# FFN loop: five mixed pairs of eight with a mixed one last, down columns copied out by ScalarE and added by GpSimd's transfers

## The chip, the cores and the metric

The kernel runs on one core of one Trainium2 chip. The metric is the device time of one execution in microseconds; several executions are timed and their median is given. A profile of one execution comes with it.

## What is computed

One block of a hybrid encoder on 256 tokens with 2048 channels: a mixer sub-layer (retention heads and a diagonal state-space group), then a dense SwiGLU feed-forward (FFN), all in float32:

```python
SEQ, D_MODEL, D_FF = 256, 2048, 5632
    x = x + mix @ w_out[l]
    h = rmsnorm(x, norm_ffn_g[l])
    x = x + (jax.nn.silu(h @ w_gate[l]) * (h @ w_up[l])) @ w_down[l]
    return rmsnorm(x, norm_final_g)
```

The change touches the last product line, the FFN.

## The kernel before

**High and low parts.** Every float32 product is made of three matmuls on rounded parts: high times high, high times low, low times high. A weight chunk (128 x 1024, 512 KB) is loaded by SyncE's queue into one of six slots (`raw`, `raw_more`), ScalarE (ACT) copies it rounded into `w_hi` (L550), VectorE (DVE) writes the rest, `raw - w_hi`, into `w_lo` (L947), and TensorE (PE) multiplies. `w_hi` and `w_lo` have four slots, so ACT may write chunk c when PE has finished chunk c-4. The semaphores `high_done`, `low_done` and `pe_done` count these steps; `ready(n)` on PE waits for `low_done` ahead of every chunk.

**The loop.** `D_FF` is cut into 11 blocks of 512. A turn (`turn(j)`, written for each engine; 10 turns) has 24 chunks. Chunks 0 to 15 are the **gate phase**: eight pairs of a gate chunk and an up chunk of the next block. Chunks 16 to 23 are the **down phase**: four columns of 512 outputs, two chunks each, of the block whose activations (`ffT`) the turn before prepared. Twelve matmuls of 512 columns per down chunk.

**Plain and mixed pairs.** The string `UNITS` says for each of the pairs 0 to 7 whether it is plain (C) or mixed (S). A plain pair takes eight block products, 24 matmuls (`plain_unit`). A mixed pair takes seven, 21 matmuls (`mixed_unit`), by sums of blocks in the way of Strassen and Winograd: first nine matmuls on three blocks of `w_hi`/`w_lo` (banks P1, P2, P3), then twelve on sums of weight blocks in `mix_hi`/`mix_lo` (banks P4 to P7). For a mixed pair DVE makes the sums (`mix_sums`, three operations, L1312 to L1317), then w_lo of one and a half chunks, then `mix_lo` (L1323, 128 x 2048); ACT makes `w_hi` of one and a half chunks and `mix_hi` (two of L559). The tile `mix` has one buffer, `mix_hi` and `mix_lo` have two. Sums of the activations (`sA`, `sB`, `sC`) are made once, ahead of the loop, by `combos`, `combo_high`, `combo_low`.

**From products to activations.** After the last mixed pair ACT copies bank P1 into `mix` (`first_product`), DVE adds P6 and P7 (`first_sums`, L1328 and L1330), and after the whole gate phase `last_sums` adds P5 and then P2 to P4 (L1336, L1339). ACT takes the silu, DVE multiplies (`ff`), turns 32 x 32 blocks (`turn_blocks`), and 16 small transfers of GpSimd's queue move them (`move`, L424); they come back as `ffT_hi` (ACT) and `ffT_lo` (DVE, L1371) in the gate phase of the next turn.

**Down columns.** The columns of the down phase use two pairs of PSUM banks in turn. When a column's two chunks are done, DVE adds both banks to the residual `x2` in SBUF (`down_add`, L1381, counted by `cols_added`), and PE may use the banks again. Each engine's queue is in program order; the order is written out by hand in `turn(j)`.

In the texts below D is the moment at which PE starts chunk 16, the first of a down phase, and T the moment at which it starts chunk 0.

Of the kernel before, what the change touches and what calls it, by code (L numbers as in the profile page):

```python
# [40 lines left out]
NCOL = 512  # L41
# [7 lines left out]
SPL = 4  # L49
# [16 lines left out]
UNITS = "CSCSSCSC"  # L66
# [3 lines left out]
B_P2, B_P3, B_P4, B_P5, B_P1, B_P6, B_P7 = range(7)  # L70
# [80 lines left out]
def build(nc, A, out):  # L151
# [20 lines left out]
    with ctx:  # L172
# [80 lines left out]
        for part, x in enumerate((m["sB_hi"], m["sB_lo"])):  # L253
            s_mixed[part] += [x[:, i] for i in range(2)]
        wbT, dec, sT = (m[k] for k in ("wbT", "dec", "sT"))
# [55 lines left out]
        d_cols_pool = [sem(f"d_cols_pool{i}") for i in range(COLS_MOVED)]  # L311
        d_last, d_last_pool = sem("d_last"), sem("d_last_pool")
# [221 lines left out]
        def _(act):  # L534
# [17 lines left out]
            def mix_high(c, turn=None):  # L552

                q = mixed_at(c)
                for half_, step in ((slice(0, 2), 1), (slice(2, 4), 3)):
                    act.wait_ge(S["mix_step"], count(turn, 3 * NM, 3 * q + step))
                    if turn is not None and step == 1:
                        act.wait_ge(S["mix_free"], count(turn, NM, q))
                    nc.scalar.activation(mix_hi[:, q % 2, half_], mix[:, half_], ACT.Copy).then_inc(S["mix_high"], 1)  # L559
# [1702 lines left out]
```

## Time and profile before

| | |
|---|---|
| median of 3 runs | 1094.39 us (1093.68 to 1094.54) |
| the profiled execution, its own time | 1094.19 us |
| its span, first to last instruction | 1092.1 us |
| busy: PE, DVE, ACT, GpSimd | 1080.7, 936.1, 601.1, 189.9 us |
| granted clock of TensorE, mean | 0.998 of full speed |

Busy time is the time in which an engine has an instruction at work; PE's matmuls overlap (a new one starts some 0.227 us after the one before, and each row lasts 0.39 us). A row of the timeline with "x2" merges two instructions. In square brackets stand the idle time ahead of an instruction and what ended it. Times count from the start of the span.

### The profile page before, as it was taken

How to read it: one execution, taken by the hardware profiler on the slowest of the kernel's cores; microseconds unless marked ns; L12 is line 12 of the kernel's file. 1: busy time of each engine (PE TensorE's matmuls, PEld its weight loads, DVE VectorE, ACT ScalarE, POOL GpSimd, SP SyncE). 2: the span in 40 equal slices, each digit the busy share in tenths (PEclk: the TensorE clock that was granted, in tenths of full speed). 3: DMA queues.
4: the chain of work that ended last, by engine and by line, in shares of the span. 5: the costliest groups of instructions: out<-in, count | busy, mean ns of one | idle time of the engine just before them, and what ended most of it. 6: DMA issues, size and time to landing. Idle time of an engine off the chain costs nothing.

```text
span 1092.1 us, 15574 instructions
## 1 busy us (share of the span) xinstructions
PE 1080.7 (99%) x5386; PEld 892.1 (82%) x5386; DVE 936.1 (86%) x1043; ACT 601.1 (55%) x738; POOL 189.9 (17%) x322
## 2 busy tenths in 40 slices
PE   9999999999999999999999999999999999999997
PEld 7878778888988888888888888888888888888886
DVE  7999998754875788989898998989899898989987
ACT  7569544445753565545555464655546465555544
POOL 7130143320100320311030302003030300303011
PEclk9999999999999999999999999999999999999999
DMA  9884588864665677666576666658566665757662
GB/s 360 286 232 147 179 235 242 268 191 150 212 218 187 205 221 229 214 206 212 197 230 220 185 228 204 201 191 241 200 210 214 207 206 182 229 192 231 214 213 113
DMA packets 123802, 232.18 MB, mean 213 GB/s; under 512 B 12016, under 2 KB 19568, under 8 KB 123120
## 3 DMA queue, kind: packets, MB, share of 16 engines
q1 hardware_dynamic: 113392, 215.10, 61.1%
q0 software_dynamic: 9952, 15.62, 5.4%
q10 hardware_dynamic: 416, 0.92, 0.2%
q8 instruction: 25, 0.41, 0.2%
q14 instruction: 17, 0.14, 0.0%
HBM read 218.09 MB, written 5.11 MB: 204 GB/s over the span
## 4 chain that ended last, share of the span: by engine, by line
PE 80%; DVE 13%; DMA 3%; issue 2%; ACT 1%; DVEq 0%; POOL 0%; SPq 0%; POOLq 0%; ACTq 0%
PE ps L1787 36%; PE ps L1751 31%; DVE w_lo L941 4%; PE ps L1778 3%; PE ps L1771 3%; PE ps L1775 3%; DMA raw<-in_w_in 2%; DVE w_lo L947 1%; DVE wb L1074 1%; DVE wb L1072 1%; ACT w_hi L544 1%; DVE wb_t L1073 1%; PE ps L2095 1%; PE ps L2096 1%; PE ps L2097 1%
## 5 line engine op out<-in xcount | busy, mean ns | idle before, releaser
L550 ACT ACTIVATE w_hi<-raw 128x1024 fp32r<-128x1024 f32 (+1 forms) x166 | 156.7, 955 | 191.2 <-PE ps L1787 117.7
L544 ACT ACTIVATE w_hi<-raw 128x1024 fp32r<-128x1024 f32 x135 | 142.7, 1060 | 154.0 <-DMA raw<-in_w_in 53.2
L941 DVE TENSOR_TENSOR w_lo<-raw,w_hi 128x1024 fp32r<-128x1024 f32 x136 | 163.8, 1220 | 63.7 <-ACT w_hi L544 63.1
L424 POOL DMA_DIRECT2D ff_moved<-ff_turned x184 | 97.0, 536 | 601.7 <-DVE ff_turned L1365 543.3
L947 DVE TENSOR_TENSOR w_lo<-raw,w_hi 128x1024 fp32r<-128x1024 f32 (+1 forms) x166 | 176.3, 1088 | 23.7 <-ACT w_hi L550 22.9
L550 ACT ACTIVATE w_hi<-raw_more 128x1024 fp32r<-128x1024 f32 x82 | 84.5, 1054 | 54.9 <-PE ps L1751 36.5
L947 DVE TENSOR_TENSOR w_lo<-raw_more,w_hi 128x1024 fp32r<-128x1024 f32 x82 | 97.4, 1218 | 8.4 <-ACT w_hi L550 8.4
L559 ACT ACTIVATE mix_hi<-mix 128x1024 fp32r<-128x1024 f32 x80 | 83.5, 1056 | 21.9 <-DVE mix L1312 15.2
L1323 DVE TENSOR_TENSOR mix_lo<-mix,mix_hi 128x2048 fp32r<-128x2048 f32 x40 | 91.4, 2285 | 0.0
L1751 PE MATMUL ps<-w_hi,ffT_hi 128*128 128x512 f32 x320 | 85.6, 389 | 0.0
L1751 PE MATMUL ps<-w_lo,ffT_hi 128*128 128x512 f32 x320 | 85.6, 389 | 0.0
L1751 PE MATMUL ps<-w_hi,ffT_lo 128*128 128x512 f32 x320 | 85.5, 389 | 0.0
L1751 PEld LDWEIGHTS ps<-w_hi,ffT_hi 128*128 128x128 f32 x320 | 60.1, 188 | 12.5
L1751 PEld LDWEIGHTS ps<-w_lo,ffT_hi 128*128 128x128 f32 x320 | 60.1, 188 | 12.5
L1751 PEld LDWEIGHTS ps<-w_hi,ffT_lo 128*128 128x128 f32 x320 | 60.1, 188 | 12.5
L1787 PE MATMUL ps<-w_hi,h2B_hi 128*128 128x512 f32 x160 | 52.8, 391 | 0.1
L1787 PE MATMUL ps<-w_lo,h2B_hi 128*128 128x512 f32 x160 | 52.9, 392 | 0.0
L1787 PE MATMUL ps<-w_hi,h2B_lo 128*128 128x512 f32 x160 | 52.9, 391 | 0.0
L1787 PE MATMUL ps<-w_lo,actA_hi 128*128 128x512 f32 x160 | 52.5, 389 | 0.0
L1787 PE MATMUL ps<-w_hi,actA_hi 128*128 128x512 f32 x160 | 52.5, 389 | 0.0
L1787 PE MATMUL ps<-w_hi,actA_lo 128*128 128x512 f32 x160 | 52.5, 389 | 0.0
L1312 DVE TENSOR_TENSOR mix<-raw 128x1024 f32<-128x1024 f32 x40 | 48.8, 1220 | 1.4 <-DMA raw<-in_w_up 0.9
(362 smaller groups left out, 2238.4 us busy)
## 6 DMA issues: line engine op xcount, KB each, us to landing
raw<-in_w_in SPq DMA_DIRECT2D x79, 512.0 KB, 5.4
raw<-in_w_gate SPq DMA_DIRECT2D x68, 512.0 KB, 3.9
raw<-in_w_up SPq DMA_DIRECT2D x68, 512.0 KB, 4.6
raw<-in_w_down SPq DMA_DIRECT2D x46, 512.0 KB, 4.1
raw_more<-in_w_down SPq DMA_DIRECT2D x42, 512.0 KB, 4.5
raw<-in_w_out SPq DMA_DIRECT2D x32, 512.0 KB, 4.1
raw_more<-in_w_gate SPq DMA_DIRECT2D x20, 512.0 KB, 4.5
raw_more<-in_w_up SPq DMA_DIRECT2D x20, 512.0 KB, 5.5
```

The lines of the kernel that those rows point to most:

```text
L424: eng.dma_start(moved[32 * b:32 * b + 32, :, a].rearrange("p t k j -> p t (k j)"), turned[32 * a:32 * a + 32, b].rearrange("p t k j -> p t ...
L544: nc.scalar.activation(w_hi[:, n % SPL], raw[:, n % RAW], ACT.Copy).then_inc(S["high_done"], 1)
L550: nc.scalar.activation(w_hi[:, c % SPL, at], raw_of(c)[:, at], ACT.Copy).then_inc(S["high_done"], 1)
L559: nc.scalar.activation(mix_hi[:, q % 2, half_], mix[:, half_], ACT.Copy).then_inc(S["mix_high"], 1)
L941: tt(w_lo[:, n % SPL], raw[:, n % RAW], w_hi[:, n % SPL].bitcast(F32), ALU.subtract).then_inc(S["low_done"], 1)
L947: tt(w_lo[:, c % SPL, at], raw_of(c)[:, at], w_hi[:, c % SPL, at].bitcast(F32), ALU.subtract).then_inc(S["low_done"], 1)
L1312: tt(mix[:, 0:2], b12.unsqueeze(1).to_broadcast([P, 2, NCOL]), blocks[:, 0::3], ALU.subtract).then_inc(S["mix_step"], 1)
L1323: tt(mix_lo[:, q % 2], mix[:], mix_hi[:, q % 2].bitcast(F32), ALU.subtract).then_inc(S["mix_low"], 1)
L1751: ins = mm(ps[:, banks + t], blocks[k][kind == 1][:, tok], w[:, s, at], start=first and kind == 0 and k == 0, stop=last and kind == 2 and ...
L1771: mm(ps[:, banks + t], blocks[k][0][:, tok], w_hi[:, s, at], start=first and k == 0, stop=False)
L1775: mm(ps[:, banks + t], blocks[k][1][:, tok], w_hi[:, s, at], start=False, stop=False)
L1787: ends[bank] = mm(ps[:, bank], x[kind == 1], w[b], start=kind == 0 and bank in fresh, stop=kind == 2 and bank in done)
```

## The change

`UNITS` becomes CSCSSCSS: pair 7 is mixed now as well, so five of eight are. Its sums of activations get tiles of their own (`sD`), and since NM is odd now, the buffers of `mix_hi`/`mix_lo` are chosen by `q % NM % 2`. The banks are dealt out anew: P1 and bank 7 are one pair of down columns, P6 and P7 the other (`COL_BANKS`). DVE no longer adds down columns; ACT copies each into `col_a` or `col_b` (`column_out`), and GpSimd's queue issues a transfer that adds it to `x2` in SBUF. The semaphore `cols_added` is called `col_done` and counts the copies, and `d_added` counts the landings of the adding transfers. `first_sums` waits for the whole gate phase (`mix_free`), and PE waits for `p1_ready` ahead of chunk 16 and for `sum_step` ahead of chunk 18 only. ACT's turn 0 is written out ahead of the loop.

```diff
-UNITS = "CSCSSCSC"
+UNITS = "CSCSSCSS"
-B_P2, B_P3, B_P4, B_P5, B_P1, B_P6, B_P7 = range(7)
+B_P2, B_P3, B_P4, B_P5, B_P6, B_P7, B_P1 = range(7)
+COL_BANKS = ((B_P1, 7), (B_P6, B_P7))
...
             def first_product(j):
 
-                act.wait_ge(S["mix_free"], j * NM + (NM + 1))
+                act.wait_ge(S["pe_done"], j * TURN + (LOOP0 + 2 * MIXED[-1] + 1))
...
+            def column_out(j, col, first=False):
+
+                act.wait_ge(S["pe_done"], j * TURN + (LOOP0 + 2 * GRP + 2 * col + 2))
+                if not (first and col < 2):
+                    act.wait_ge(d_added[col % 2], j * 32 + 16 * (col // 2))
+                nc.scalar.activation(col_out[col % 2][:], column_psum(col), ACT.Copy).then_inc(S["col_done"], 1)
...
+                    if c in (2 * GRP + 5, 2 * GRP + 7, TURN + 1):
+                        column_out(j, (c - 2 * GRP - 5) // 2, first)
+                    if c == TURN + 3:
+                        column_out(j, 3, first)
...
             def first_sums(j):
 
                 dve.wait_ge(S["p1_ready"], j + 1)
+                dve.wait_ge(S["mix_free"], j * NM + (NM + 1))
...
-            def down_col(chunks, before, c):
-
-
-                dve.wait_ge(S["pe_done"], chunks)
-                dve.wait_ge(S["cols_added"], before)
-                b0 = 6 - 2 * (c % 2)
-                cols = x2[:, :, NCOL * c:NCOL * (c + 1)]
-                tt(cols, ps[:, b0:b0 + 2], cols, ALU.add).then_inc(S["cols_added"], 1)
...
             for j in range(FG - 1):
                 pool.wait_ge(S["turned"], j + (COLS_MOVED + 1))
                 move(pool, PAIRS, ff_turned, ff_moved, d_moved)
-            pool.wait_ge(S["turned"], COLS_MOVED + FG)
-            pool.wait_ge(S["ffT_lo_ready"], FG - 1)
-            move(pool, PAIRS[8:], ff_turned, ff_moved, d_last_pool)
+                for col in range(4):
+                    pool.wait_ge(S["col_done"], 4 * j + 9 + col)
+                    pool.dma_start(x2[:, :, NCOL * col:NCOL * (col + 1)], col_out[col % 2][:], accum_op=ALU.add
+                                   ).then_inc(d_added[col % 2], 16)
...
                 for c in range(2 * GRP, TURN):
                     col, k = divmod(c - 2 * GRP, 2)
                     if c == 2 * GRP:
                         pe.wait_ge(S["ffT_lo_ready"], j + 1)
+                        pe.wait_ge(S["p1_ready"], j + 1)
+                    if c == 2 * GRP + 2:
                         pe.wait_ge(S["sum_step"], j * 4 + 2)
```

Two places in the order of the instructions matter below. The first is DVE's queue at the hand-over from the gate phase to the down phase, in the loop's body. The first row is the w_lo of chunk 17, and the two rows behind the sums are those of chunks 18 and 19. Before:

```order
L947 TENSOR_TENSOR w_lo<-raw_more,w_hi 128x1024 [waits high_done]
L1328 TENSOR_TENSOR mix<-ps,mix 128x512 [waits p1_ready]
L1330 TENSOR_TENSOR mix<-ps,mix 128x512 [waits sum_step]
L1336 TENSOR_TENSOR mix<-mix,ps 128x2x512 [waits sum_step,pe_done]
L1339 TENSOR_TENSOR mix<-ps,mix 128x1536 [waits sum_step]
L946 REGISTER_ALU
L947 TENSOR_TENSOR w_lo<-raw,w_hi 128x1024 [waits high_done]
L946 REGISTER_ALU
L947 TENSOR_TENSOR w_lo<-raw,w_hi 128x1024 [waits high_done]
```

The changed kernel has the same instructions there, under other line numbers:

```order
L977 TENSOR_TENSOR w_lo<-raw_more,w_hi 128x1024 [waits high_done]
L1364 REGISTER_ALU [waits p1_ready]
L1365 TENSOR_TENSOR mix<-ps,mix 128x512 [waits mix_free]
L1366 ISA
L1367 TENSOR_TENSOR mix<-ps,mix 128x512 [waits sum_step]
L1372 REGISTER_ALU [waits pe_done]
L1373 TENSOR_TENSOR mix<-mix,ps 128x2x512 [waits sum_step]
L1375 REGISTER_ALU
L1376 TENSOR_TENSOR mix<-ps,mix 128x1536 [waits sum_step]
L976 REGISTER_ALU
L977 TENSOR_TENSOR w_lo<-raw,w_hi 128x1024 [waits high_done]
```

The order has not moved, but the first of the four sums waits for `mix_free` now, which the last matmul of pair 7 gives; before, the first wait of the four for the end of pair 7 was that of the third (`pe_done`, L1336).

The second place is ACT's queue in the down phase, between the silu and the next turn. The rows of `w_hi` are chunks 20 to 23 and then 0 and 1 of the next turn. The changed kernel, in the turn that is written out:

```order
L885 ACTIVATE ff_act<-mix,rstd 128x512
L569 ACTIVATE w_hi<-raw 128x1024 [waits pe_done,d_raw2]
L569 ACTIVATE w_hi<-raw 128x1024 [waits pe_done,d_raw3]
L893 ACTIVATE col_a<-ps 128x1024 [waits pe_done]
L569 ACTIVATE w_hi<-raw_more 128x1024 [waits pe_done,d_raw4]
L569 ACTIVATE w_hi<-raw_more 128x1024 [waits pe_done,d_raw5]
L893 ACTIVATE col_b<-ps 128x1024 [waits pe_done]
L569 ACTIVATE w_hi<-raw 128x1024 [waits pe_done,d_raw0]
L569 ACTIVATE w_hi<-raw 128x1024 [waits pe_done,d_raw1]
L893 ACTIVATE col_a<-ps 128x1024 [waits d_added0,pe_done]
```

The rows of L893 are new, each behind the `w_hi` of two chunks; the third waits for the landing of the first column's adding transfer as well. The fourth stands behind the two `mix_hi` of the next turn's pair 1.

## Rows read from the trace of the kernel before

**Rows 1.** The page, part 1: busy us of each engine (share) xinstructions.

```profile
PE 1080.7 (99%) x5386; PEld 892.1 (82%) x5386; DVE 936.1 (86%) x1043; ACT 601.1 (55%) x738; POOL 189.9 (17%) x322
```

**Rows 2.** The chain that ended last: start us, us, what, one turn.

```profile
560.24 41.08 PE ps L1787 x180
601.32 21.76 PE ps L1751 x96
```

**Rows 3.** Windows, one turn: us, busy (x) of five engines, PEclk, DMA share, GB/s.

```profile
560.24:623.08 62.84, 62.84 (x277) 51.84 (x277) 56.90 (x54) 34.02 (x36) 8.41 (x16) 1.00 0.65 208
```

**Rows 4.** Timeline of PE, one turn: start us, us, what.

```profile
590.82 0.62 PE L1787 MATMUL ps<-w_hi,h2B_hi 128*128 128x512 f32 x2
...
595.69 0.62 PE L1787 MATMUL ps<-w_hi,h2B_hi 128*128 128x512 f32 x2
...
601.16 1.07 PE L1751 MATMUL ps<-w_hi,ffT_hi 128*128 128x512 f32 x4
...
606.60 1.07 PE L1751 MATMUL ps<-w_hi,ffT_hi 128*128 128x512 f32 x4
```

**Rows 5.** Groups of DVE in the same turn, shapes apart.

```profile
L1381 DVE TENSOR_TENSOR x<-ps,x 128x1024 f32<-128x1024 f32 x4 | 4.9, 1216 | 0.0
```

**Rows 6.** Timeline of DVE at the same hand-over, from 597 us.

```profile
597.42 0.68 DVE L1328 TENSOR_TENSOR mix<-ps,mix 128x512 f32<-128x512 f32 x1
598.14 0.69 DVE L1330 TENSOR_TENSOR mix<-ps,mix 128x512 f32<-128x512 f32 x1
601.36 1.22 DVE L1336 TENSOR_TENSOR mix<-mix,ps 128x1024 f32<-128x1024 f32 x1 [2.53 <-PE ps L1787]
602.61 1.76 DVE L1339 TENSOR_TENSOR mix<-ps,mix 128x1536 f32<-128x1536 f32 x1
604.29 2.35 DVE L947 TENSOR_TENSOR w_lo<-raw,w_hi 128x1024 fp32r<-128x1024 f32 x2
```

**Rows 7.** Timeline of DVE in turn 0, at pair 4.

```profile
452.68 1.82 DVE L947 TENSOR_TENSOR w_lo<-raw,w_hi 128x1024 fp32r<-128x1024 f32 x2
```

**Rows 8.** Timeline of PE at the same place.

```profile
454.04 0.39 PE L1787 MATMUL ps<-mix_lo,actA_hi 128*128 128x512 f32 x1
...
455.13 0.39 PE L1787 MATMUL ps<-w_hi,sB_hi 128*128 128x512 f32 x1
```

**Rows 9.** Timeline of DVE, pair 6 of a later turn.

```profile
646.42 1.22 DVE L1312 TENSOR_TENSOR mix<-raw 128x1024 f32<-128x1024 f32 x1
...
649.01 1.82 DVE L947 TENSOR_TENSOR w_lo<-raw,w_hi 128x1024 fp32r<-128x1024 f32 x2
650.75 2.29 DVE L1323 TENSOR_TENSOR mix_lo<-mix,mix_hi 128x2048 fp32r<-128x2048 f32 x1
652.95 1.22 DVE L947 TENSOR_TENSOR w_lo<-raw,w_hi 128x1024 fp32r<-128x1024 f32 x1
```

**Rows 10.** Timeline of ACT, around the start and end of a gate phase.

```profile
623.65 1.99 ACT L559 ACTIVATE mix_hi<-mix 128x1024 fp32r<-128x1024 f32 x2
625.84 1.07 ACT L550 ACTIVATE w_hi<-raw_more 128x1024 fp32r<-128x1024 f32 x1 [0.19 <-PE ps L1787]
...
653.86 1.06 ACT L550 ACTIVATE w_hi<-raw 128x1024 fp32r<-128x1024 f32 x1 [1.66 <-PE ps L1787]
```

**Rows 11.** Timeline of DVE ahead of turn 0.

```profile
423.45 0.28 DVE L1286 TENSOR_TENSOR s_sum<-h_sum 128x128 f32<-128x128 f32 x1
...
424.71 1.22 DVE L941 TENSOR_TENSOR w_lo<-raw,w_hi 128x1024 fp32r<-128x1024 f32 x1
...
428.50 0.42 DVE L1299 TENSOR_TENSOR sC_lo<-s_sum,sC_hi 128x256 fp32r<-128x256 f32 x1
...
432.12 1.23 DVE L1312 TENSOR_TENSOR mix<-raw 128x1024 f32<-128x1024 f32 x1 [0.94 <-DMA raw<-in_w_up]
```

**Rows 12.** DMA issues of the execution: KB each, median us to landing.

```profile
u_scratch<-uT POOLq DMA_DIRECT2D x2, 512.0 KB, 5.1
...
x<-in_x_tok SPq DMA_DIRECT2D x1, 2048.0 KB, 9.0
```

More of the change, by code:

```diff
@@ L254, in build @@
             s_mixed[part] += [x[:, i] for i in range(2)]
+        for part in range(2):
+            s_mixed[part].append(s_last[part][:])
         wbT, dec, sT = (m[k] for k in ("wbT", "dec", "sT"))
@@ L363, in mixed_pair, with combo_parts @@
             return c % TURN < 2 * GRP and c % TURN // 2 in MIXED
-        def column_combos(c):
-            one = 2 * c if 2 * c in MIXED else 2 * c + 1
-            return MIXED.index(one), PLAIN.index(4 * c + 1 - one), one - 2 * c
+        def combo_parts(c):
+            first, parts = 0, []
+            for u in (2 * c, 2 * c + 1):
+                width = 4 if u in MIXED else 2
+                to = [s_mixed[part][MIXED.index(u)] if u in MIXED else s_plain[part][PLAIN.index(u)] for part in range(2)]
+                parts.append((s_sum[:, first:first + width], to))
+                first += width
+            return parts
         def act_block(kb, part):
@@ L557, in mix_high @@
                     if turn is not None and step == 1:
[L558 to L559 removed]
+                        act.wait_ge(S["mix_free"], count(turn, NM, q + (NM % 2 and q == NM)))
+                    nc.scalar.activation(mix_hi[:, q % NM % 2, half_], mix[:, half_], ACT.Copy).then_inc(S["mix_high"], 1)
             def pair_high(c, turn=None):
@@ L883, in _, with turn @@
                 pair_high(c)
-            def turn(j, last=False):
+            def turn(j, first=False, last=False):
                 for c in range(SPL, TURN + SPL):
@@ L902, in turn @@
                                              ).then_inc(S["ffT_hi_ready"], 1)
-            with act.Fori(0, FG - 2) as j:
+            turn(0, first=True)
+            with act.Fori(1, FG - 2) as j:
                 turn(j)
@@ L1277, in combos @@
             def combos(c):
-                _, _, one = column_combos(c)
                 pair = h_sum[:].rearrange("p (u k) (t s) -> p u k t s", u=2, t=TOK)
-                (a11, a21), (a12, a22) = ([pair[:, one, k, t] for t in range(TOK)] for k in range(2))
-                plain = pair[:, 1 - one]
-                dve.wait_ge(S["h_summed"], 3 * c + 1)
+                done = sum(1 + 2 * (u in MIXED) for u in range(2 * c)) - c
+                dve.wait_ge(S["h_summed"], done + 1)
                 if c:
@@ new lines, in combos @@
+                for i, (sums, _) in enumerate(combo_parts(c)):
+                    if 2 * c + i in MIXED:
+                        a11, a21, a12, a22 = (pair[:, i, k, t] for k in range(2) for t in range(TOK))
+                        tt(sums[:, 0], a21, a22, ALU.add).then_inc(S["h_summed"], 1)
+                        tt(sums[:, 2], a21, a11, ALU.subtract)
+                        mixed.append((sums, a11, a12))
+                    else:
+                        last = tt(sums, pair[:, i, :, 0], pair[:, i, :, 1], ALU.subtract)
@@ L1294, in combo_low @@
+                for i, (sums, a11, _) in enumerate(mixed):
+                    dve.wait_ge(S["h_summed"], done + 2 + i)
+                    tt(sums[:, 1], sums[:, 0], a11, ALU.subtract).then_inc(S["h_summed"], 1)
+                for i, (sums, _, a12) in enumerate(mixed):
+                    dve.wait_ge(S["h_summed"], done + 2 + len(mixed) + i)
+                    last = tt(sums[:, 3], a12, sums[:, 1], ALU.subtract)
+                last.then_inc(S["s_summed"], 1)
             def combo_low(c):
-                i, k, _ = column_combos(c)
```

95 lines of the change are left out of this document (47 added, 48 removed).

## The prediction

> **What bounds the kernel now.** I read the page first: PE is busy 99% of the span, DVE 86%, ACT 55% [rows 1]. So a stretch of PE's work saved is worth its full length only as long as DVE, the next engine, keeps its deadlines. The chain of work that ended last says the same for the loop: one turn after another is two pieces, both PE, 41.08 us of gate phase and 21.76 us of down phase, with nothing between [rows 2]. The windows of that turn put 56.90 us of DVE's work and 34.02 us of ACT's into 62.84 us, and the sixteen DMA engines are busy 0.65 of it, 41 us [rows 3]. PE does not wait in these turns; DVE is ahead of it by a margin that differs from place to place. The question is therefore which margin the change uses up, and I walk through one turn for that.
>
> **What is removed: three matmuls a turn.** Pair 7 goes from 24 matmuls to 21. Pair 6 is a mixed pair on the same activations (h2B) and lasts from 590.82 to 595.69, 4.87 us; pair 7, plain, lasts to 601.16, 5.47 us [rows 4]. That is 0.60 us. At the usual step of a matmul (5.44 us for the 24 of the first down column, 601.16 to 606.60 [rows 4], 0.227 each) it would be 0.68. I take 0.64 a turn, 6.4 us in ten turns, with 6.0 and 6.8 as ends.
>
> **DVE's work.** It loses four down adds of 1.22 us, 4.9 us a turn [rows 5]. It gains the mixed pair's work. For pair 6 that is 2.59 us of sums (646.42 to 649.01), 1.74 us of w_lo and 2.20 us of `mix_lo` (starts at 649.01, 650.75, 652.95) [rows 9], 6.53 us, where a plain pair needs two w_lo of 1.2 us [rows 9]. Net +4.1 -4.9: DVE's sum hardly moves and PE's turn gets 0.6 shorter. By sums alone the change would pay in full.
>
> **The hand-over to the down phase.** This is where it does not. Today `first_sums` runs at 597.42 and 598.14, while PE is in pair 7; DVE then idles 2.53 us until pair 7's end lets `last_sums` start at 601.36, 0.20 us after PE's chunk 16 starts (D = 601.16) [rows 4, 6]. The two last sums take until 604.29, then come the w_lo of chunks 18 and 19, the first done at about 605.51. PE wants chunk 18 at 606.60: a margin of 1.1 us.
> With pair 7 mixed, P6 and P7 end with pair 7's last matmul, so the first of the four sums cannot start before D + 0.20. The chain behind it is serial and each step is in the rows: 0.72 (597.42 to 598.14), 0.72 again for the second (the same operation, followed by one that waits for it), 2.93 for the two last sums (601.36 to 604.29), 1.22 for w_lo 18: D + 0.20 + 0.72 + 0.72 + 2.93 + 1.22 = D + 5.79. PE wants it at D + 5.44. The work that hid the first two sums was pair 7; now nothing does.
> What such a lateness costs is seen once in the trace, in turn 0 at pair 4: w_lo was complete at 452.68 + 1.82 = 454.50 [rows 7]. PE's last matmul before it started at 454.04, so the next chunk was due at 454.27 and its third matmul at 454.72; it started at 455.13 [rows 8]. Late by 0.23, lost 0.41: the loss is the lateness plus 0.18. Here: 0.35 + 0.18 = **0.53 us a turn**, 5.3 us in ten turns. I take 0.45 to 0.65 as its ends, for a step may differ by a few hundredths. PE cannot make up for it later, since everything behind is its own work.
> Other deadlines there hold. `p1_ready`: P1 ends after nine of pair 7's 21 matmuls, so ACT's copy of one bank can start 2.7 us (twelve matmuls) ahead of D. Chunk 19 is due at D + 8.7, its w_lo is ready at D + 6.9. The columns of P6 and P7 are free at about D + 1.7, before chunk 18.
>
> **Pair 7 as a mixed pair.** DVE is free at 652.95, after pair 6's `mix_lo` [rows 9]. Sums to 655.5, w_lo to 657.3, `mix_lo` to 659.5. PE starts pair 7 at 595.69 + 62.84 = 658.53 and its second half nine matmuls later, about 660.6. Margins 1.2 and 1.1 us: tight, but no wait. ACT does not spoil it: its `w_hi` 15 starts at 653.86 by PE's release [rows 10], now half as long, and the two `mix_hi` end a microsecond behind the sums, before DVE needs them. Then w_lo 16, `ffT_lo` and w_lo 17 take DVE to about 662.9, PE's new D being 663.4: in time.
>
> **ACT's copies.** Four a turn; the 128 x 1024 copy is 1.06 us where the source is SBUF [rows 10], and I take the same from PSUM. With `mix_hi` (two, 2.0 us) less half a `w_hi` ACT gains some 6 us on 34 in 62: its sum is no bound. Three copies stand where it waited for PE anyway. The fourth stands behind the `mix_hi` of pair 1, which end at 625.64; the `w_hi` of chunk 4 started at 625.84 [rows 10] and now starts at 626.7. The w_lo of chunk 5 comes when PE releases its slot, as before, and so costs nothing. PE needs the fourth column's banks only in pair 1's second half, at T + 7.5; the copy is over at T + 3.8.
>
> **The adding transfers.** Nothing in the trace adds while it moves, so I bound it. Below: a plain transfer of the same 512 KB from GpSimd's queue lands in 5.1 us; above: one of four times the bytes in 9.0 us [rows 12]. An adding transfer reads source and target and writes, so I take 7 us, between the two. The first deadline is the third column's copy, which waits for the first column's landing. Column 0 is complete at D + 5.4, and ACT, after silu and two `w_hi`, has copied it by D + 9; ACT wants to copy column 2 at about D + 18, after PE's chunk 21 and its own `w_hi`. So 9 us, and 1.5 more in which ACT would be idle: hidden. The fourth waits for the second with 12 us. In GpSimd's queue the 16 moves of the next block now stand behind the fourth add, some 13 us later than today; they end by about T + 15, and `ffT_hi` reads them at T + 32: hidden.
> The Trainium skill, "DMA: Bandwidth & Descriptors", section "Issuing engines are not separate DMA queues", says that transfers of all queues interleave on the same 16 engines, so the adds compete with the weights. By the fit in its section on the SWDGE path (2.0 us plus bytes over 436 GB/s) half a megabyte would be an estimate of 3.2 us, and 4.4 with the target's read; no run here shows an adding transfer yet. By it the rival of slow adds would be out; by the rows above it is open.
>
> **Ahead of turn 0.** The last group of sums has two mixed pairs: eight small operations where five take 1.26 us, and a w_lo of 512 columns where 256 take 0.33 (428.50 to the next operation), so DVE gets about 0.7 us later there. It waits only 0.94 us for a transfer, and that is released by the w_lo just before, so it shifts too [rows 11]. In turn 0 PE does wait for DVE at pair 4 [rows 8], so this comes through, and at pair 7 DVE has less reserve than later (a mixed pair costs it 6.5 us, PE 4.9), worth 0.2 to 1. I take +1.1 for both, ends 0.4 and 1.8.
>
> **The sum.** Against the profiled execution's own 1094.19 us: -6.4 (matmuls) +5.3 (wait at chunk 18) +1.1 (turn 0) = 1094.2. That execution stands 0.2 below the median of the runs, so I say 1094.3: no change. The ends of the terms give -6.8 + 4.5 + 0.4 = -1.9 and -6.0 + 6.5 + 1.8 = +2.3, so 1092.3 to 1096.6 for this case, practically all within 0.2% (2.2 us), which is also about what a measurement of this kernel can tell from no change. The tail after the last turn is the same work, and its waits for the landings have over 8 us.
>
> **The rivals.**
> - *The wait does not come* (the sums are quicker out of PSUM, or PE's deadline is later than I read it). For it: 0.35 us of lateness is small against a turn. Against it: every step is a row of this kernel, and 0.4 us in a chain of 5.8 would have to vanish. Time: 1094.2 - 5.3 = 1088.9.
> - *The margins at the mixed pairs go too.* Pair 7's 1.1 us, and those of pair 4, which follows pair 3 the same way. If weights land a microsecond or two later under the adds, the sums of pair 1 start later and DVE, which runs without a pause from there to pair 6, hands it on. Price: 0.4 us a turn, 4 us: 1098.
> - *Slow adds, the case on the slower side.* One mechanism: ACT, in order, waits for the first column's landing before its third copy, and all `w_hi` behind it wait. It decides from about 10.5 us from copy to landing, or from (62.2 - 41)/4 = 5.3 us of all sixteen DMA engines for each add. At 12.5 us of landing it costs 2 us a turn, 20 us: 1114.
> - That the adds take work from DVE but DVE's sum is no bound is not a rival but part of the forecast: taking them away shortens nothing by itself.
>
> **How the numbers follow.** Forecast 0.46, no wait 0.19, margins gone 0.17, slow adds 0.14; 0.04 for something between (half the wait) that ends faster. Range 1088.5 to 1100: it takes in the first three and leaves out the slow adds and a little more. Faster: 0.19 + 0.04 + 0.01 of the forecast's low end = 0.24. Slower: 0.17 + 0.14, less 0.01 that stays within = 0.30. Within 0.2%: 0.46.
>
> **What would show it.** In the changed kernel's trace PE should idle, ten times, about 0.5 us at the third down chunk behind DVE's w_lo, and four sums should stand in one row right behind the first down matmul. Gate phases should be 40.4 to 40.5 us long, the down phases 22.3. The adds should land in 5 to 9 us and no ACT row should name them as releaser. I am wrong if the down phase is 21.8 us still, if a wait for `mix_lo` or w_lo stands at pair 4 or 7 of every turn, or if ACT waits for the adds.

## The result: 0.4% slower, the loop as forecast and the tail not

| | before | after |
|---|---|---|
| median of 6 runs each | 1094.38 us (1093.68 to 1094.81) | 1099.25 us (1098.30 to 1100.84) |
| ratio, with 95% interval | | 1.0041 (1.0030 to 1.0051) |
| profiled execution: its own time, span | 1094.19, 1092.1 us | 1099.47, 1097.5 us |

The kernel is 4.9 us slower. The time lies inside the range on record, but the forecast case, no change, did not come, and the kernel is on the side that had 0.30. In the changed kernel the names of the lines are: L1774 down matmuls (L1751 before), L1810 mixed gate matmuls (L1787), L977 `w_lo` (L947), L1365 to L1376 the four sums, L893 `column_out`, L1730 the adding transfer.

Busy time of the changed kernel, the page's part 1, answers to [rows 1]:

```profile
PE 1079.6 (98%) x5356; PEld 887.2 (81%) x5356; DVE 935.9 (85%) x1046; ACT 647.8 (59%) x798; POOL 240.7 (22%) x362
```

Thirty matmuls are gone, three in each of ten turns, and DVE's sum has not moved. One turn in the chain that ended last (start us, us, what), beside [rows 2]:

```profile
560.29 40.41 PE ps L1810 x177
...
600.73 0.70 DVE mix L1365
...
602.18 1.23 DVE mix L1373
...
605.11 1.22 DVE w_lo L977
...
606.38 16.61 PE ps L1774 x72
```

What the reader is to see: the gate phase shrank from 41.08 to 40.41 us, and what was one unbroken piece of 21.76 us of PE is now interrupted after two chunks. The chain leaves PE at 600.7, goes through DVE's sums and the w_lo of chunk 18, and returns to PE at 606.38. PE's timeline there, beside [rows 4], says the same from PE's side:

```profile
600.53 1.07 PE L1774 MATMUL ps<-w_hi,ffT_hi 128*128 128x512 f32 x4
...
606.38 1.20 PE L1774 MATMUL ps<-w_hi,ffT_hi 128*128 128x512 f32 x4 [0.25 <-DVE w_lo L977]
```

Chunk 18 starts at D + 5.85 (606.38 - 600.53) where 5.44 was due. That is 0.41 us late, and the first four matmuls behind it take 0.13 longer than the row of chunk 16 (1.20 against 1.07). The idle time in the brackets (0.25) is smaller than the loss, for the matmul before still counts as busy in a part of the wait. From 600.70, the end of the gate phase in the chain, to the next gate phase at 623.00 it is 22.29 us, 0.53 more than 21.76.

The same turn in the windows (us, busy of five engines, PEclk, DMA share, GB/s), beside [rows 3]:

```profile
497.60:560.29 62.69, 62.44 (x274) 51.21 (x274) 56.87 (x54) 38.68 (x42) 13.37 (x20) 1.00 0.81 242
```

ACT has 4.7 us more, GpSimd 5.0, and the sixteen DMA engines went from 0.65 to 0.81 of the turn. PE waits for none of these.

To place the 4.9 us I cut both spans at the same four points: the start of the loop (433.87 and 432.96 us), the start of turn 1 (497.24 and 497.43), the moment at which the tail's first chunk was due (1062.80 and 1061.99), and the end. All are starts of matmuls in PE's timeline, which stand 0.16 us ahead of the chain's marks (601.16 there is 601.32 in the chain of [rows 2]).

| us | before | after | difference |
|---|---|---|---|
| up to the loop | 433.87 | 432.96 | -0.9 |
| turn 0 | 63.37 | 64.47 | +1.1 |
| nine more turns | 565.56 | 564.56 | -1.0 |
| the tail | 29.3 | 35.5 | +6.2 |
| span | 1092.1 | 1097.5 | +5.4 |

These are single executions, and the first two rows vary between executions: in the profiles of e1, e4 and e8 (below), whose kernels are the changed one up to the tail, the loop starts at 433.95, 433.56 and 432.98 us and turn 0 lasts 64.87, 64.37 and 65.60. The nine turns do not vary so (564.53 us in e1), and 6.2 us are well beyond this scatter. So turns and tail have to be told apart: the turns did what was forecast, and the loss lies in the last 36 us. In the tail block 10 of the FFN is finished: eight more chunks of down weights against `ffE_hi`/`ffE_lo`, and the final norm, for which 1 MB `g_final` is loaded. PE's timeline of the changed kernel there:

```profile
1063.52 1.17 PE L1774 MATMUL ps<-w_hi,ffE_hi 128*128 128x512 f32 x4 [1.37 <-issue]
...
1077.39 0.50 PE L1763 MATMUL ps<-w_hi,ffE_hi 128*128 128x512 f32 x1 [2.71 <-DVE x L1555]
```

Two waits. The first chunk starts 1.5 us after it was due (1061.99), the fifth 2.9 us after (1074.52). What DVE and ACT waited for ahead of them, from their timelines:

```profile
1061.10 1.06 ACT L930 ACTIVATE ffE_hi<-ff_moved 128x1024 fp32r<-128x1024 f32 x1 [2.32 <-DMA ff_moved<-ff_turned]
...
1077.15 1.06 ACT L569 ACTIVATE w_hi<-raw 128x1024 fp32r<-128x1024 f32 x1 [6.57 <-DMA raw<-in_w_down]
```

```profile
1073.77 2.36 DVE L977 TENSOR_TENSOR w_lo<-raw_more,w_hi 128x1024 fp32r<-128x1024 f32 x2 [7.40 <-DMA g_final<-in_g_final]
```

Everything late there is a landing: the moved blocks, `g_final`, the weights of the last chunks. The DMA issues of the last turn and the tail (KB each, median us to landing), before and then after:

```profile
raw_more<-in_w_down SPq DMA_DIRECT2D x2, 512.0 KB, 6.2
g_final<-in_g_final SPq DMA_DIRECT2D x1, 1024.0 KB, 8.6
...
ff_moved<-ff_turned SPq DMA_DIRECT2D x8, 32.0 KB, 2.3
```

```profile
x<-col_a POOLq DMA_DIRECT2D x2, 512.0 KB, 9.2
raw_more<-in_w_down SPq DMA_DIRECT2D x2, 512.0 KB, 8.6
g_final<-in_g_final SPq DMA_DIRECT2D x1, 1024.0 KB, 13.4
ff_moved<-ff_turned SPq DMA_DIRECT2D x8, 32.0 KB, 4.2
```

The windows of the same stretch, again before and then after:

```profile
1046.00:1062.80 16.80, 16.80 (x76) 13.89 (x75) 15.15 (x16) 7.95 (x8) 4.22 (x8) 1.00 0.77 240
1062.80:1078.00 15.20, 15.20 (x69) 12.59 (x68) 12.50 (x14) 7.75 (x12) 0.00 (x0) 1.00 0.29 117
```

```profile
1046.00:1063.50 17.50, 16.15 (x72) 13.01 (x71) 11.43 (x13) 10.56 (x11) 8.00 (x11) 1.00 0.90 214
1063.50:1078.40 14.90, 12.17 (x52) 9.79 (x53) 6.87 (x7) 5.16 (x5) 1.19 (x1) 1.00 0.94 278
```

From 1046 to 1078 the DMA engines had 17.3 us of work (0.77 x 16.80 + 0.29 x 15.20) and have 29.8 (0.90 x 17.50 + 0.94 x 14.90) in 32.4 us. They are nearly full. The page's part 3 (queue: packets, MB, share of 16 engines) gives the price of one adding transfer; first the lines of before, then of after:

```profile
q1 hardware_dynamic: 113392, 215.10, 61.1%
q0 software_dynamic: 9952, 15.62, 5.4%
```

```profile
q1 hardware_dynamic: 113392, 215.10, 59.5%
q0 software_dynamic: 20832, 36.59, 15.8%
```

0.158 x 1097.5 less 0.054 x 1092.1 is 114 us for 40 transfers, 2.9 us of all sixteen engines for each. That is the upper end: q1's time fell by 14 us for the same bytes, so both queues together grew by 100 us, 2.5 for each. Four of them are 10 to 11.4 us, most of the 12.5 that this stretch has more.

A third piece is PE's own. Two windows of the changed kernel, the stretch without a matmul and the one behind it:

```profile
1074.68:1077.39 2.71, 0.00 (x0) 0.00 (x1) 2.68 (x5) 0.24 (x1) 0.00 (x0) 1.00 0.74 260
1077.39:1082.50 5.11, 5.11 (x15) 4.06 (x16) 5.11 (x6) 4.61 (x10) 0.00 (x0) 0.67 0.01 3
```

After 2.71 us in which PE stood, the granted clock of the next 5.1 us is 0.67: part of the stretch ran at the lower of TensorE's two levels, 1.2 instead of 2.4 GHz. Eight matmuls between 1078.58 and 1081.99 follow each other at 0.43 us instead of 0.23, 1.6 us lost. Late start 1.5, late fifth chunk 2.9 and the clock 1.6 make 6.0 of the tail's 6.2 us. The clock's part is not the same in every execution, as e2 and e3 show below.

### The profile page after: what moved, and what is told of

Read it like the earlier page. It is cut to its first block, busy times and chain, and to the rows that moved or that the text cites. A ratio compares the mean times of both kernels' runs of the same rounds, so it can differ in the third digit from the quotient of the medians.

```text
span 1097.5 us, 15723 instructions
## 1 busy us (share of the span) xinstructions
PE 1079.6 (98%) x5356; PEld 887.2 (81%) x5356; DVE 935.9 (85%) x1046; ACT 647.8 (59%) x798; POOL 240.7 (22%) x362
## 3 DMA queue, kind: packets, MB, share of 16 engines
q1 hardware_dynamic: 113392, 215.10, 59.5%
q0 software_dynamic: 20832, 36.59, 15.8%
HBM read 218.09 MB, written 5.11 MB: 203 GB/s over the span
## 4 chain that ended last, share of the span: by engine, by line
PE 75%; DVE 15%; issue 4%; DMA 4%; ACT 1%; SPq 0%; DVEq 0%; POOL 0%; POOLq 0%; ACTq 0%
PE ps L1810 33%; PE ps L1774 27%; PE ps L1801 3%; PE ps L1794 3%; PE ps L1798 3%; DVE w_lo L971 3%; DVE w_lo L977 2%; DMA raw<-in_w_in 2%; DMA g_final<-in_g_final 1%; DVE mix L1373 1%; DVE mix_lo L1359 1%; DVE mix L1367 1%; DVE mix L1365 1%; PE ps L2120 1%; PE ps L2121 1%
## 5 line engine op out<-in xcount | busy, mean ns | idle before, releaser
L569 ACT ACTIVATE w_hi<-raw 128x1024 fp32r<-128x1024 f32 (+1 forms) x166 | 150.0, 927 | 141.3 <-PE ps L1810 84.2
L977 DVE TENSOR_TENSOR w_lo<-raw,w_hi 128x1024 fp32r<-128x1024 f32 (+1 forms) x166 | 171.0, 1056 | 30.7 <-ACT w_hi L569 30.1
L1359 DVE TENSOR_TENSOR mix_lo<-mix,mix_hi 128x2048 fp32r<-128x2048 f32 x50 | 114.3, 2285 | 10.8 <-ACT mix_hi L578 10.8
L443 POOL DMA_DIRECT2D ff_moved<-ff_turned x184 | 102.5, 865 | 78.3 <-DVE ff_turned L1402 77.9
L578 ACT ACTIVATE mix_hi<-mix 128x1024 fp32r<-128x1024 f32 x100 | 103.6, 1054 | 22.4 <-DVE mix L1348 13.4
L1730 POOL DMA_DIRECT2D x<-col_a x20 | 24.4, 1222 | 398.5 <-ACT col_a L893 393.3
L977 DVE TENSOR_TENSOR w_lo<-raw_more,w_hi 128x1024 fp32r<-128x1024 f32 x82 | 98.2, 1217 | 12.3 <-DMA g_final<-in_g_final 7.4
L1774 PE MATMUL ps<-w_hi,ffT_hi 128*128 128x512 f32 x320 | 86.8, 393 | 2.9 <-DVE w_lo L977 2.9
L1774 PE MATMUL ps<-w_hi,ffT_lo 128*128 128x512 f32 x320 | 85.6, 390 | 0.0
L1774 PE MATMUL ps<-w_lo,ffT_hi 128*128 128x512 f32 x320 | 85.6, 389 | 0.0
L1774 PEld LDWEIGHTS ps<-w_hi,ffT_hi 128*128 128x128 f32 x320 | 59.3, 188 | 18.9 <-DVE w_lo L977 6.2
L1774 PEld LDWEIGHTS ps<-w_hi,ffT_lo 128*128 128x128 f32 x320 | 60.1, 188 | 12.6
L1774 PEld LDWEIGHTS ps<-w_lo,ffT_hi 128*128 128x128 f32 x320 | 60.1, 188 | 12.5
L1348 DVE TENSOR_TENSOR mix<-raw 128x1024 f32<-128x1024 f32 x50 | 61.0, 1221 | 1.7 <-DMA raw<-in_w_up 0.8
L1810 PE MATMUL ps<-w_hi,actA_hi 128*128 128x512 f32 x160 | 52.7, 390 | 0.1
L1810 PE MATMUL ps<-w_lo,actA_hi 128*128 128x512 f32 x160 | 52.5, 389 | 0.0
L1810 PE MATMUL ps<-w_hi,actA_lo 128*128 128x512 f32 x160 | 52.5, 389 | 0.0
L1794 PE MATMUL ps<-w_hi,actA_hi 128*128 128x512 f32 x160 | 44.6, 401 | 0.1
L1794 PE MATMUL ps<-w_hi,actB_hi 128*128 128x512 f32 x160 | 44.3, 399 | 0.0
```

The lines of the kernel that those rows point to most:

```text
L443: eng.dma_start(moved[32 * b:32 * b + 32, :, a].rearrange("p t k j -> p t (k j)"), turned[32 * a:32 * a + 32, b].rearrange("p t k j -> p t ...
L569: nc.scalar.activation(w_hi[:, c % SPL, at], raw_of(c)[:, at], ACT.Copy).then_inc(S["high_done"], 1)
L578: nc.scalar.activation(mix_hi[:, q % NM % 2, half_], mix[:, half_], ACT.Copy).then_inc(S["mix_high"], 1)
L977: tt(w_lo[:, c % SPL, at], raw_of(c)[:, at], w_hi[:, c % SPL, at].bitcast(F32), ALU.subtract).then_inc(S["low_done"], 1)
L1348: tt(mix[:, 0:2], b12.unsqueeze(1).to_broadcast([P, 2, NCOL]), blocks[:, 0::3], ALU.subtract).then_inc(S["mix_step"], 1)
L1359: tt(mix_lo[:, q % NM % 2], mix[:], mix_hi[:, q % NM % 2].bitcast(F32), ALU.subtract).then_inc(S["mix_low"], 1)
```

## The experiments

Each row is the median of a kernel's runs against the kernel before in the same series (1094.43 us for the first four, 1094.33 for the last four), with the ratio and its interval. Each kernel starts from the changed one.

| kernel | us | ratio |
|---|---|---|
| e1_gfin_late | 1098.82 | 1.0039 (1.0028 to 1.0050) |
| e2_low18_first | 1093.91 | 0.9995 (0.9985 to 1.0004) |
| e3_four_mixed | 1098.60 | 1.0032 (1.0020 to 1.0044) |
| e4_no_last_adds | 1094.14 | 0.9994 (0.9984 to 1.0004) |
| e5_plain | 1095.35 | 1.0008 (0.9999 to 1.0017) |
| e6_dve_last | 1089.26 | 0.9951 (0.9937 to 0.9964) |
| e7_dve_adds | 1090.27 | 0.9965 (0.9951 to 0.9978) |
| e8_gfin_last | 1100.62 | 1.0055 (1.0040 to 1.0071) |

**e4_no_last_adds: is it these four transfers?** The adding transfers of the last turn (j = 9) are left out, and so the down columns of that turn are missing from `x2`; the 36 of the other turns stay. The waits for the four landings go with them (not shown in the cut).

```diff
-                    pool.dma_start(x2[:, :, NCOL * col:NCOL * (col + 1)], col_out[col % 2][:], accum_op=ALU.add
+                    if j < FG - 2:
+                      pool.dma_start(x2[:, :, NCOL * col:NCOL * (col + 1)], col_out[col % 2][:], accum_op=ALU.add
```

> The changed kernel without the adding transfers of the last turn (four of forty; the last turn's down columns are copied out and left out of the result). Theory: these four cause all of the tail's loss, by both ways, the late moves (1.4 us at the first tail chunk) and the late loads (2.9 plus 1.7): the tail takes 29.3 us again, and the time is 1099.2 - 6.1 = 1093.1 to 1093.5. Rival: the tail's loss comes from elsewhere (order of waits, the ScalarE copies): over 1097.

Measured 1094.14, 5.1 below the changed kernel, a little less than the 5.7 to 6.1 expected. In its tail PE has no wait at all, and the tail takes 29.3 us, as before. The windows of its last stretch:

```profile
1046.00:1062.00 16.00, 15.98 (x71) 13.25 (x72) 12.38 (x13) 10.94 (x12) 4.26 (x8) 1.00 0.71 224
1062.00:1078.00 16.00, 16.00 (x72) 13.28 (x71) 11.75 (x13) 9.00 (x14) 0.19 (x1) 1.00 0.35 138
```

The DMA engines are back at 17.0 us of work, and `g_final` lands in 7.9 us. Even the issuing gets shorter. SyncE's queue issues eight of the moves in one row; in the changed kernel and in this one:

```profile
1050.23 8.13 SPq L443 DMA_DIRECT2D ff_moved<-ff_turned  x8
```

```profile
1050.71 5.12 SPq L443 DMA_DIRECT2D ff_moved<-ff_turned  x8
```

Weights and `g_final` stand behind them in that queue, so they are both issued later (`g_final` at 1060.40 instead of 1057.53 us) and land later. The whole tail loss hangs on four of the forty transfers.

**e3_four_mixed: what do copies and transfers cost without the fifth mixed pair?** `UNITS` is CSCSSCSC again (`sC` with four tiles and no `sD`); banks, copies and adding transfers stay.

```diff
-UNITS = "CSCSSCSS"
+UNITS = "CSCSSCSC"
```

> The changed kernel with pair 7 plain again (four mixed pairs, as before), so that only the copies by ScalarE, the adding transfers and the new banks remain. Theory: in the turns the adds are hidden, period 62.84 us as before, and the tail's loss of some 6 us is theirs alone: about 1100.2. Rival: if the adding transfers cost in the turns as well, the period is above 62.9 and the time above 1101; if the tail's loss needs the fifth mixed pair, the time is 1094.4.

Measured 1098.60. Its turns, in the chain that ended last:

```profile
500.78 41.08 PE ps L1807 x180
541.86 21.76 PE ps L1771 x96
```

That is 62.84 us, [rows 2] to the hundredth: behind turn 0 the copies and adding transfers cost the turns nothing. The time is 1.6 us below the 1100.2 expected, and it is neither rival's. The profiled execution was one of its longer ones (1101.92), with a span 8.0 us above that of the kernel before: 4.6 of them are in the tail, 2.5 in turn 0 (65.89 us, with waits of 0.99, 0.42 and 0.44 for DVE's w_lo) and 0.9 ahead of the loop. So the tail loses without the fifth mixed pair too, but how the median's 4.2 us are split is not shown.

**e2_low18_first: the wait at chunk 18.** DVE makes the w_lo of chunk 18 ahead of the four sums.

```diff
                 loop_low(d + 1, j)
+                loop_low(d + 2, j)
                 first_sums(j)
                 last_sums(j)
-                loop_low(d + 2, j)
```

> The changed kernel, with one edit: DVE writes the w_lo of chunk 18 ahead of first_sums instead of behind last_sums. Theory: PE's wait of 0.53 us at the third down chunk of each turn is the serial chain of four sums and w_lo 18 behind the end of pair 7; with w_lo 18 ahead of it the wait goes in all ten turns, loop period 62.16 to 62.2 us instead of 62.70, time 1099.2 - 5.3 = 1094.0, the tail unchanged. Rival: the wait moves to chunk 19 or to ACT's silu, and less than half comes back, over 1096.5.

Measured 1093.91, 5.3 below the changed kernel, which is the term of the sum. A turn is 40.40 + 21.76 = 62.16 us:

```profile
560.38 40.40 PE ps L1810 x177
600.78 21.76 PE ps L1774 x96
```

The tail's two waits are still there, the fifth chunk's as 2.41 us behind the same DVE row. But the clock does not fall behind it. In the tail of e3 it falls behind a shorter wait at the same chunk, 1.86 us. The windows behind these two waits, e2 and then e3:

```profile
1073.00:1078.10 5.10, 4.75 (x20) 3.63 (x21) 5.10 (x6) 4.60 (x10) 0.00 (x0) 1.00 0.01 3
```

```profile
1079.90:1085.00 5.10, 5.06 (x15) 4.06 (x16) 4.77 (x6) 4.18 (x8) 0.00 (x0) 0.67 0.07 24
```

**e1_gfin_late: is it `g_final`?** The trace names `g_final` for the larger wait. DVE waits for it once, ahead of the w_lo of the tail's fifth chunk, by a wait that stands earlier than its first use (behind that w_lo and the next stands the add, L1555, that gives PE its banks and is named in PE's row). I moved the wait down to that use.

```diff
             def gain_col(col):
                 at = slice(NCOL * col, NCOL * (col + 1))
                 dve.wait_ge(S["last_added"], 2 * col + 2)
+                if col == 0:
+                    dve.wait_ge(d_gfin, 16)
...
-            dve.wait_ge(d_gfin, 16)
```

> The changed kernel, with one edit: DVE's wait for the load of g_final stands ahead of its first use in the tail (gain_col of column 0) and no longer ahead of the w_lo of tail chunk 4. Theory: the adding transfers of the last turn make the tail's loads late, and g_final, landing after 13.4 us instead of 8.6, is what PE waits 2.9 us for, with 1.7 us more at half clock behind it. If that wait is all, the time falls by 4.6 to about 1094.7. If the weights of tail chunks 6 and 7, which landed 16 us after their issue, are late in any case, PE waits for them instead, at the first matmul of column 3, about 2 us, and the time falls by only 1.5 to 3, to about 1097. Rival (the loss lies in the turns, not the tail): no change, 1099.2.

A miss: 1098.82, 0.4 less than the changed kernel, which is within the noise, where 1.5 to 4.6 were expected. The wait for `g_final` at the fifth chunk is gone, and two shorter ones stand 2.3 and 4.6 us later. PE's and then ACT's timeline:

```profile
1079.70 0.50 PE L1764 MATMUL ps<-w_hi,ffE_hi 128*128 128x512 f32 x1 [0.76 <-DVE w_lo L977]
...
1082.03 0.50 PE L1764 MATMUL ps<-w_hi,ffE_hi 128*128 128x512 f32 x1 [0.68 <-DVE w_lo L977]
```

```profile
1077.33 1.06 ACT L569 ACTIVATE w_hi<-raw 128x1024 fp32r<-128x1024 f32 x1 [5.39 <-DMA raw<-in_w_down]
```

The last section of PE's work goes by halves of the tokens, so chunks five and six serve twelve matmuls and then PE asks for chunks seven and eight. The weights of the seventh become available at the same 1077 us as in the changed kernel. In this execution the tail was 33.1 us, 2.4 shorter than the changed kernel's, with no lower clock, but it began 1.4 us later; the median of eight runs kept only 0.4. The name of the releaser was right and the cause wrong: `g_final` was one of several landings that were late together.

**e8_gfin_last: a better order of the loads?** With the wait of e1, and the load of `g_final` issued behind the last two weight chunks instead of ahead of them.

```diff
-            sp.wait_ge(S["mix_free"], 1 + NM * (FG - 1))
-            sp.dma_start(g_final[:], A["g_final"]).then_inc(d_gfin, 16)
...
             for c in range(RING, GRP):
                 sp.wait_ge(S["low_done"], TAIL0 + c - RING + 1)
                 refill(c, down(FG - 1, c + 2 * GRP))
+            sp.wait_ge(S["mix_free"], 1 + NM * (FG - 1))
+            sp.dma_start(g_final[:], A["g_final"]).then_inc(d_gfin, 16)
```

> The changed kernel with DVE's wait for g_final moved to its first use (as in the first experiment) and the load of g_final issued behind the weights of tail chunks 6 and 7 instead of ahead of them. Theory: with the wait moved, PE waited for the weights of chunks 6 and 7, which land late because 1 MB of g_final and the last adds share the engines with them; without g_final ahead they land some 3 us earlier and the time falls from 1098.8 to about 1096.5. Rival: the order on the queue does not matter, only the adds do: 1098.8.

A miss in the other direction: 1100.62, the slowest of all. Now `g_final`, issued last, lands after 15.9 us, DVE's first use of it stands ahead of the w_lo of the seventh chunk, and PE waits longer. DVE's and PE's timeline, and two windows:

```profile
1079.59 1.22 DVE L1564 TENSOR_TENSOR x_gain<-x,g_final 128x1024 f32<-128x1024 f32 x1 [5.48 <-DMA g_final<-in_g_final]
```

```profile
1082.00 0.50 PE L1764 MATMUL ps<-w_hi,ffE_hi 128*128 128x512 f32 x1 [3.51 <-DVE w_lo L977]
```

```profile
1064.61:1078.49 13.88, 13.88 (x60) 11.15 (x60) 5.91 (x6) 6.79 (x8) 1.19 (x1) 1.00 1.01 298
...
1082.00:1087.00 5.00, 4.32 (x12) 3.22 (x13) 4.71 (x6) 2.17 (x6) 1.52 (x3) 0.65 0.00 0
1087.00:1092.00 5.00, 5.00 (x19) 4.06 (x18) 1.82 (x3) 0.72 (x2) 0.87 (x3) 0.66 0.00 0
```

In all three orders (the changed kernel, e1, e8) the DMA engines are nearly full from the tail's start (0.90 to 1.01 of the windows) and run dry only at about 1077 to 1079 us. I read that as a sum, not an order: something that PE needs before then comes last, whichever it is. Each of the three runs shows only its own order. Inside the first of the last two windows stands a second wait, of 0.68 us. The profile of e8 is of an execution that was 3 us above its median, so it may have lost more by the lower clock than the usual run.

**e5_plain: bytes, or adding?** All forty transfers are plain copies of the same bytes (`accum_op` left out), so `x2` is overwritten by the last turn's columns.

```diff
-                    pool.dma_start(x2[:, :, NCOL * col:NCOL * (col + 1)], col_out[col % 2][:], accum_op=ALU.add
+                    pool.dma_start(x2[:, :, NCOL * col:NCOL * (col + 1)], col_out[col % 2][:]
```

> The changed kernel with its forty adding transfers made plain ones of the same size (they overwrite x2 instead of adding to it, so the down products but the last are lost from the result). Theory: what hurts the tail is that an adding transfer holds the DMA engines for longer than a plain one (q0 rose from 5.4% to 15.8% of sixteen engines for 21 MB, 5.4 us per MB, where the weights take 3.0); plain, they land in some 5 us instead of 9, the tail loses half of its 6 us, about 1096. Rival: the bytes and the queueing alone do it, adding costs nothing more: landing 8 to 9 us, 1099.

Measured 1095.35, 3.9 below the changed kernel. The page's part 3, and the answer for the transfers' line, first the landing with adding, then the plain one:

```profile
q0 software_dynamic: 15712, 36.59, 10.4%
```

```profile
L1730 POOL DMA_DIRECT2D x<-col_a x20: 1191/1221/1263, 484.3 to 1059.1; - x20
...
DMA to landing us min/median/max: 5.9/8.9/10.4
```

```profile
L1730 POOL DMA_DIRECT2D x<-col_a x20: 722/728/742, 486.3 to 1061.0; - x20
...
DMA to landing us min/median/max: 3.2/5.9/8.6
```

The same bytes take 0.104 x 1094.0 less 59 us, 54.8 us for 40, 1.37 us of sixteen engines each: adding doubles it to 2.9 (by all queues together, 1.24 and 2.5). It also takes 1.22 us instead of 0.73 on GpSimd and lands in 8.9 instead of 5.9 us. With plain copies the tail's waits shrink to one of 0.33 us, and none is at the first chunk. That tells two causes apart. The moves of SyncE's queue still land after 4.3 us (4.2 in the changed kernel), and the engines are 0.95 busy while they are issued, but the issuing is short again:

```profile
1052.19 5.14 SPq L443 DMA_DIRECT2D ff_moved<-ff_turned  x8
```

So the first chunk's 1.5 us in the changed kernel go with the 3.0 us that the issuing takes longer; the longer landing alone makes no wait there.

**e6_dve_last: keep what pays.** w_lo of chunk 18 first (e2), and in the last turn alone DVE adds the copied columns from `col_a` and `col_b` to `x2` in SBUF instead of a transfer (four operations of 1.2 us, `last_col`, between the w_lo of the tail's first chunks).

```diff
+            def last_col(col):
+                dve.wait_ge(S["col_done"], 4 * (FG - 2) + 9 + col)
+                dve.wait_ge(d_added[col % 2], 32 * (FG - 2))
+                cols = x2[:, :, NCOL * col:NCOL * (col + 1)]
+                tt(cols, col_out[col % 2][:], cols, ALU.add).then_inc(S["col_added"], 1)
...
+                    last_col(0)
                     loop_low(TURN, j)
+                    last_col(1)
                     loop_low(TURN + 1, j)
```

> Both losses taken away: w_lo of chunk 18 ahead of first_sums, and in the last turn DVE adds the copied columns to x2 in SBUF (four 128x1024 operations in its idle time), so that no adding transfer meets the tail's loads. Theory: 1094.1 of the run without last adds less the 5.3 of the chunk 18 wait: 1088.8, 0.5% faster than before. Rival (another wait appears once these two are gone): over 1091.

Measured 1089.26, near the 1088.8 expected: 5.1 us faster than the kernel before, 10.0 than the changed one, the lowest median of all. Both losses are gone; gate phase, and then 144 down matmuls of the last turn and the tail in one piece:

```profile
621.78 40.40 PE ps L1822 x177
...
1035.14 32.64 PE ps L1786 x144
```

**e7_dve_adds: were the transfers needed at all?** w_lo of chunk 18 first, five mixed pairs, and DVE adds every down column out of PSUM as in the kernel before: no copies, no adding transfers.

```diff
+            def down_add(j, col):
+                dve.wait_ge(S["pe_done"], j * TURN + (LOOP0 + 2 * GRP + 2 * col + 2))
+                dve.wait_ge(S["col_done"], j * 4 + (col + 5))
+                cols = x2[:, :, NCOL * col:NCOL * (col + 1)]
+                tt(cols, column_psum(col), cols, ALU.add).then_inc(S["col_done"], 1)
```

> Five mixed pairs with the new banks and w_lo of chunk 18 ahead of first_sums, but the down columns added by DVE out of PSUM as before: no copies by ScalarE, no adding transfers. Theory: DVE's four adds fit, because in the down phase it is held by ACT and PE anyway (its idle 1.5 us ahead of w_lo 25 stays) and only the margins at pair 7 shrink by 0.2: period 62.2 us, no loss in the tail, 1088.8. Rival: DVE's sum (61 of 62.2 us) no longer fits, PE waits at the mixed pairs or down chunks, period 62.8 or more and time 1095 or more; then the transfers were needed.

Measured 1090.27, 1.5 above the forecast and far from the rival's 1095, 4.1 us faster than the kernel before. One turn in the windows, and for comparison one of e6:

```profile
560.27:622.43 62.16, 62.16 (x275) 51.26 (x274) 60.98 (x58) 35.19 (x38) 8.44 (x16) 1.00 0.66 210
```

```profile
559.62:621.78 62.16, 62.16 (x274) 51.26 (x274) 56.56 (x53) 39.15 (x42) 13.44 (x20) 1.00 0.83 246
```

DVE is at work for 60.98 of 62.16 us and PE still never waits: the turn is as long as with the transfers. By the medians of five runs each the transfers bring 1.0 us over e7; the ranges overlap (1087.94 to 1089.45 and 1089.08 to 1091.18), and so do the intervals of the ratios. The profiled e6 is 0.65 us ahead at 560 us (the starts of the two windows), and e7 has two short waits in turn 0 (0.34 and 0.20 us) that e6 hasn't. But e2, whose kernel is e6's up to the last turn, starts that turn at 560.38 and has such a wait (0.44) as well. So the 1.0 us is not placed, and whether the transfers bring anything is open.

## Why the prediction was half right

- **The matmuls removed, 0.64 a turn: right.** The gate phase went from 41.08 to 40.41, 0.67; 0.60 to 0.68 was given.
- **The hand-over, 0.53 a turn: right.** Its two parts, 0.35 late and 0.18 on top, measured 0.41 and 0.12; that the sum agrees to the hundredth is luck. The down phase is 22.29 against 21.76, the four sums stand in one row from D + 0.20, chunk 18 waits for DVE's w_lo, ten times. e2 took it away and gave back 5.3 us.
- **Margins at the mixed pairs and ACT's copies: right.** No turn behind turn 0 has a wait there; the rival that priced this at 1098 met the time by chance and did not happen.
- **Turn 0, +1.1: within its ends in the profiled execution, its cause not shown.** The working has -0.64 + 0.53 + 1.1 = +1.0 for turn 0, and the trace +1.1; but PE began it 0.9 us earlier, so that turn 1 starts only 0.2 later than before. The small operations ahead of it are longer, as forecast (1.62 us where 1.26 stood, and 0.61 for 0.33), yet DVE starts the first sum of pair 1 at 431.96, not later than the 432.12 of before. The other profiles spread by over a microsecond there, and the longest turn 0, 65.89, is that of e3, which has four mixed pairs.
- **The landing, 7 us: too low, without effect.** 5.9 to 10.4, median 8.9, where 5.1 and 9.0 were the bounds. ACT had 9 us and 1.5 of slack and never waited for it in a turn, though the longest landing came within 0.1 us of their sum. The estimates from the Trainium skill, "DMA: Bandwidth & Descriptors", in its section on the SWDGE path, were 3.2 and 4.4 us; the plain copies' fastest landing is 3.2, their median 5.9, the adding ones' 8.9. Here, beside the weights, only the fastest plain landing met the fit.
- **The slow adds, 1114: no.** The engines' time for one is at most 2.9 us, against the 5.3 from which it would have decided, and a turn at 0.81 has room for four.
- **The step that failed** is the last sentence of the sum: "The tail after the last turn is the same work, and its waits for the landings have over 8 us." I had looked there only for who waits for the adding transfers, found DVE's waits with 8 us in hand, and they do hold. I did not ask what else the transfers are in the way of. The DMA engines are shared, the four adds of the last turn fall between 1048.8 and about 1075 us, and that is where the tail's moves, two of its weight chunks and `g_final` must land for deadlines that come once and cannot slide. I had weighed the sharing of the engines (the Trainium skill, "DMA: Bandwidth & Descriptors", section "Issuing engines are not separate DMA queues", states that transfers of all queues interleave, and the trace agrees: SyncE's moves land in 4.2 us instead of 2.3 beside GpSimd's adds) but put it into the turns, where 0.65 was taken. A tail's DMA demand is its own sum: 17 us of work in 32 before, 30 after. The tail stood in the sum at nothing; it measured +6.2 in the profiled execution and 5.1 by e4. With +5 the sum gives 1099.3, where 1099.25 was measured; so close a hit is luck too, since the parts ahead of turn 1 moved by a microsecond from one execution to the next.

e4, e5 and e6 show this from three sides: without the four transfers, with the forty at half their engine time, and with the four turned into DVE's work, the kernel takes 5.1, 3.9 and (e6 against e2) 4.7 us less. e1 and e8 show that no order of the loads that I tried avoids it. e5 shows for the first chunk that the late start goes with the longer issuing in SyncE's queue. Not shown: how much of the fifth chunk's 2.9 us is from loads that are issued later and how much from their longer landing.

## What to carry to other kernels

Sum up the DMA engines' work not over the loop but in every stretch with deadlines of its own, the last turn and the tail above all: a transfer that costs nothing in nine turns can cost 5 us in the last one, and there an engine with idle time can do the work. When a wait names one transfer, ask what all transfers of that stretch add up to before moving the one; if the engines are busy without a break, another takes its place. And where a mixed or fused step takes away the work that covered a serial chain, look in the queue for one item that doesn't depend on the chain and is needed first: one line moved here was worth 5.3 us.

## What the hardware showed that I had not expected

- A transfer that adds 512 KB from SBUF into SBUF holds the sixteen engines 2.5 to 2.9 us, a plain one 1.2 to 1.4; a weight chunk of the same size from HBM 1.6 (0.595 x 1097.5 us for 215.10 MB, times 0.524 MB). It is issued in 1.22 instead of 0.73 us and counts 272 packets instead of 144 (20832, 15712 and 9952 of queue q0, over 40 transfers).
- Beside adding transfers issuing gets slower on another queue as well: eight moves of SyncE's queue take 7.22 to 8.59 us in the five profiles with adding transfers in the last turn (the changed kernel, e1, e2, e3, e8) and 5.11 to 5.14 in the five without (before, e4, e5, e6, e7). Full engines alone don't do it: in e5 they are 0.95 busy meanwhile.
- The granted clock after PE has stood: 1.00 behind waits of 1.56, 0.76 and 0.68 us (e1) and behind one of 2.41 us (e2); 0.67 in the 5.1 us behind waits of 2.71 us (the changed kernel) and 1.86 us (e3); 0.65 in ten microseconds behind waits of 3.51 and 0.68 us (e8). In the changed kernel the fall cost 1.6 us on top of the wait. The length of the wait alone does not decide it here, for the clock held behind 2.41 us and fell behind 1.86. What does is not shown.
